# RMS and layer norms before products: turning undivided blocks by transposes, and applying the deviations behind the products

## The reference, cut to what matters

```
def rms_norm(x, g):
    y = xf * lax.rsqrt(jnp.mean(xf * xf, axis=-1, keepdims=True) + EPS)
    return (y * g.astype(jnp.float32)).astype(x.dtype)

def swiglu(h, w_gate, w_up, w_down):
    return (jax.nn.silu(h @ w_gate) * (h @ w_up)) @ w_down

def second_block(x, ...):
    h = swiglu(rms_norm(x, ff1_norm_pre[l]), ff1_w_gate[l], ff1_w_up[l], ff1_w_down[l])
    x = x + 0.5 * rms_norm(h, ff1_norm_post[l])
    h = hybrid_mixer(rms_norm(x, mix_norm_pre[l]), w_in[l], ...)
    x = x + rms_norm(h, mix_norm_post[l])
    h = swiglu(rms_norm(x, ff2_norm_pre[l]), ff2_w_gate[l], ff2_w_up[l], ff2_w_down[l])
    x = x + 0.5 * rms_norm(h, ff2_norm_post[l])
```

## Time and profile before

| | |
|---|---|
| median of the runs | 2370.24 us |
| profiled execution, its own time | 2373.72 us |
| its span, first to last instruction | 2371.5 us |
| TensorE matmul busy | 2320.2 us, 98% |
| VectorE, ScalarE, GpSimd busy | 890.4, 966.3, 988.9 us |
| mean granted TensorE clock | 0.996 |

### The profile page before, as it was taken

The page is one execution under the profiler, slowest core; times in us unless marked ns, Lnnn a source line. Parts: engine busy times, 40 slices in busy tenths (PEclk is TensorE's granted clock), DMA queues, the critical chain, the costliest instruction groups (busy, mean ns, idle before and its releaser), DMA issues.

```text
span 2371.5 us, 30775 instructions
## 1 busy us (share of the span) xinstructions
PE 2320.2 (98%) x11388; PEld 1906.8 (80%) x11388; DVE 890.4 (38%) x1181; ACT 966.3 (41%) x1643; POOL 988.9 (42%) x444
## 2 busy tenths in 40 slices
PE   8989999999999999999999999999999999999998
PEld 6868888888888878888887888888878768888887
DVE  6974444420453433444303322200536762323201
ACT  6775333321455553333314422222445565322212
POOL 6945444444322325444443444444343203444443
PEclk9999999999999999999999999999999999999999
DMA  5213322222212133222222222222321002322222
GB/s 187 72 49 104 114 97 97 97 98 94 84 63 68 58 115 107 98 97 97 90 96 89 94 94 96 97 98 98 142 72 62 28 15 76 106 97 97 95 94 95
DMA packets 58757, 215.20 MB, mean 91 GB/s; under 512 B 6448, under 2 KB 6448, under 8 KB 58416
## 3 DMA queue, kind: packets, MB, share of 16 engines
q1 hardware_dynamic: 55440, 199.83, 24.2%
q10 hardware_dynamic: 3232, 14.16, 1.6%
HBM read 211.86 MB, written 2.10 MB: 90 GB/s over the span
## 4 chain that ended last, share of the span: by engine, by line
PE 59%; issue 22%; POOL 10%; DVE 5%; ACT 3%; DMA 1%; POOLq 0%; SPq 0%; DVEq 0%; ACTq 0%
PE banks L510 12%; PE banks L512 12%; PE banks L511 12%; POOL wL L458 9%; PE banks L536 6%; PE banks L537 6%; PE banks L538 6%; DVE banks L1929 2%; PE banks L993 1%; POOL pool_sum L473 1%; PE banks L1037 1%; DMA raw<-ws 1%; PE banks L551 1%; ACT tmp L1661 1%; PE banks L945 0%
## 5 line engine op out<-in xcount | busy, mean ns | idle before, releaser
L458 POOL TENSOR_TENSOR wL<-raw,wH 128x1024 fp32r<-128x1024 f32 x369 | 898.1, 2436 | 1355.9 <-ACT wH L1202 1355.7
L1202 ACT ACTIVATE wH<-raw 128x1024 fp32r<-128x1024 f32 x371 | 393.5, 1061 | 1088.5 <-PE banks L512 598.6
L510 PE MATMUL banks<-xH,wH 128*128 128x512 f32 (+1 forms) x1976 | 762.5, 386 | 13.6 <-DVE xL L1751 10.8
L512 PE MATMUL banks<-xH,wL 128*128 128x512 f32 (+1 forms) x1976 | 756.1, 383 | 0.0
L511 PE MATMUL banks<-xL,wH 128*128 128x512 f32 (+1 forms) x1976 | 756.0, 383 | 0.0
L510 PEld LDWEIGHTS banks<-xH,wH 128*128 128x128 f32 x1976 | 371.8, 188 | 90.8 <-DVE wL L1756 10.8
L512 PEld LDWEIGHTS banks<-xH,wL 128*128 128x128 f32 x1976 | 371.8, 188 | 72.8
L511 PEld LDWEIGHTS banks<-xL,wH 128*128 128x128 f32 x1976 | 371.9, 188 | 72.0 <-issue 1.0
L536 PE MATMUL banks<-wH,hH 128*128 128x512 f32 x704 | 274.2, 389 | 3.5 <-DVE tmp L1888 3.5
L537 PE MATMUL banks<-wH,hL 128*128 128x512 f32 x704 | 273.9, 389 | 0.0
L538 PE MATMUL banks<-wL,hH 128*128 128x512 f32 x704 | 273.9, 389 | 0.0
(11 more groups left out here) (282 smaller groups left out, 2287.0 us busy)
## 6 DMA issues: line engine op xcount, KB each, us to landing
raw<-ws SPq DMA_DIRECT2D x371, 512.0 KB, 3.2
w1b<-w ACTq DMA_DIRECT2D x2, 2048.0 KB, 10.7
tmp<-rows ACTq DMA_DIRECT2D x7, 512.0 KB, 3.4
b_row<-rows ACTq DMA_DIRECT2D x5, 512.0 KB, 3.8
tmp<-xT SPq DMA_DIRECT2D x8, 256.0 KB, 7.3
xr<-xN ACTq DMA_DIRECT2D x1, 2048.0 KB, 8.6
out<-xr SPq DMA_DIRECT2D x4, 512.0 KB, 2.6
pf<-pT ACTq DMA_DIRECT2D x2, 512.0 KB, 3.3
```

The costliest lines, as they stand in the source:

```text
L458: pool.tensor_tensor(wL[:, j, :], raw[:, j, :], fp(wH[:, j, :]), ALU.subtract).then_inc(low_ready, 1)
L510: pe.matmul(bank, wH[:, slot, cols], rh, start=start, stop=False)
L512: return pe.matmul(bank, wL[:, slot, cols], rh, start=False, stop=stop)
L1202: act.activation(wH[:, c % SLOTS, :], raw[:, c % SLOTS, :], ACT.Copy).then_inc(high_ready, 1)
```

## The change

At the four places a block is turned by plain transposes (`pe.transpose` with the identity), and `turner` and `turning_matrix` are gone.

- Layer norm at `ffn0`: ScalarE divides the block in place before it is turned (`divide_block`), and VectorE later only adds the bias row (`shift_block` for `finish_block`).
- The three RMS norms before a product: the undivided `xr` is turned as soon as VectorE has finished the block. `pre_block` still computes 1/deviation, but nothing before the product waits for it. TensorE later spreads the four columns over a row of 512 tokens in bank 3 (`spread`, four transposes of a column read 128 times), and VectorE copies it to `r_row` (`take_row`).
- The factor is applied behind the products: to the gate's bank by VectorE before silu (44 products of 128x512, new semaphore `gate_scaled`), in the mixer to the copied and turned items and to the rotary tables themselves, once. The up product stays unscaled. Its factor is applied at the layer's end: as `scale` in the square of `post_block`, and in `update_block` together with the gain row (`SCALE_OF`).
- Orders are changed: `pre_block` of blocks 1, or 2 and 3, stands later on ScalarE, and VectorE makes all casts of the first half before it takes in block 3.

```diff
             def turn_block(xname, q, src):
                 h = q // 2
-                pe.wait_ge(x_normed, QT * TURN[xname] + q + 1)
                 for n in range(KT):
                     bank = ps[TURN_BANKS[xname][h][n // 2]]
                     o = (n % 2) * 2 * P + (q % 2) * P
-                    if src is divided:
-                        mm = pe.transpose(bank[:, o:o + P], xg[:, q, n * P:n * P + P], cc("ident"))
-                    else:
-                        mm = pe.matmul(bank[:, o:o + P], src(q)[:, n * P:n * P + P], turner[:, q, :], start=True, stop=True)
+                    mm = pe.transpose(bank[:, o:o + P], src[:, q, n * P:n * P + P], cc("ident"))
...
+            def updated(xname, q):
+                if xname == "ff1_pre":
+                    pe.wait_ge(res_step, RES_STEPS[2] + q + 1)
+                else:
+                    name = {"mix_pre": "down2", "ff2_pre": "wout"}[xname]
+                    pe.wait_ge(block_taken, 8 * FULL[name] + 2 * q + 2)
+                turn_block(xname, q, xr)
+
+            def spread(name, xname):
+                for q in range(QT):
+                    pe.wait_ge(x_normed, QT * TURN[xname] + q + 1)
+                    mm = pe.transpose(ps[3][:, q * P:q * P + P], figure(name, q, 7).broadcast_to([P, P]), cc("ident"))
+                mm.then_inc(r_turned, 1)
...
-                gate_and_up(1, c0 + 2)
+                if inst < 2:
+                    gate_and_up(1, c0 + 2)
+                else:
+                    tile_product(ps[6][:], c0 + 2, (c0 + 2) % SLOTS)
+                    spread(*(("down1", "ff1_pre") if inst == 2 else ("wout", "ff2_pre")))
+                    tile_product(ps[7][:], c0 + 3, (c0 + 3) % SLOTS)
...
@@ scalar, layer_norm (ffn0) and pre_block
-                    unit_block(name, q)
+                    divide_block(name, q)
...
-                turning_matrix(name, q, 7)
+                act.sem_inc(x_normed, 1)
...
@@ scalar, down1 to gateup2
             pre_block("down1", "ff1_pre", 0)
+            high_tiles("ff1_pre", 0, 0, 2, gain="ff1_pre")
+            deviation("down1", 2)
+            high_tiles("ff1_pre", 0, 2, 4, gain="ff1_pre")
+            deviation("down1", 3)
             pre_block("down1", "ff1_pre", 1)
-            deviation("down1", 2)
-            high_tiles("ff1_pre", 0, 0, 2, gain="ff1_pre")
-            deviation("down1", 3)
-            high_tiles("ff1_pre", 0, 2, 4, gain="ff1_pre")
+            high_after(CHUNK["gateup2"] - 1)
+            high_tiles("ff1_pre", 1, 0, 4, gain="ff1_pre")
             pre_block("down1", "ff1_pre", 2)
             pre_block("down1", "ff1_pre", 3)
-            high_after(CHUNK["gateup2"] - 1)
-            high_tiles("ff1_pre", 1, 0, 4, gain="ff1_pre")
...
@@ vector, ffn
+                        else:
+                            dve.wait_ge(chunk_done, t * 4 + (c0 + 2 * j + 1))
+                            dve.wait_ge(h_made, t * 2 + (24 * inst + j + 1))
+                            dve.tensor_tensor(tmp[:, j, :], ps[4 + 2 * j][:], r_row[:], ALU.mult).then_inc(gate_scaled, 1)
...
@@ vector, mixer
+            take_row("mix_pre")
             take_item(0)
             take_item(1)
+            dve.wait_ge(rope_loaded, 16)
+            for a in range(2):
+                dve.tensor_tensor(ropeT[:, a, :], ropeT[:, a, :], r_row[:], ALU.mult).then_inc(rope_scaled, 1)
```

More of the change, by code:

```diff
@@ L263, in build_block @@
         x_turned = sem("x_turned")
+        r_turned = sem("r_turned")
+        r_ready = sem("r_ready")
+        gate_scaled = sem("gate_scaled")
         res_step = sem("res_step")
@@ L400, in build_block @@
             TURN_BANKS[n] = ((0, 1, 2, 3), (6, 7, 0, 1))
+        PRE_ROW = {n: i for i, n in enumerate(["ff1_pre", "mix_pre", "ff2_pre"])}
+        SCALE_OF = {"down2": "down1", "down3": "wout"}
         XV = {"in": 0, "mix0": KT, "ffn0": 3 * KT, "mix1": 5 * KT, "ff1_pre": 7 * KT, "mix_pre": 9 * KT,
@@ L912, in last_pair @@
                 begin_wo(1, range(LEAD))
-            first_chunks((ps[7], ps[6]), c0, "down0", "ffn0", centred("down0"), (4, 6), 3)
+            first_chunks((ps[7], ps[6]), c0, "down0", "ffn0", divided, (4, 6), 3)
             project(0, 0, 2)
@@ L1123, in _ @@
             first_chunks((ps[item_bank(0)], ps[item_bank(1)]), c0, "down2", "mix_pre", updated, (4, 8), 8)
+            spread("down2", "mix_pre")
             project_item(2)
@@ L1312, in post_block @@
                     act.wait_ge(chunk_done, CHUNK[name] + dict(COUNTS)[name])
-                act.activation(squares[:], banks[:, 2 * q:2 * q + 2, :].rearrange("p a b -> p (a b)"), ACT.Square,
-                               accum_out=figure(name, q, 3)).then_inc(post_sum, 1)
+                block = banks[:, 2 * q:2 * q + 2, :].rearrange("p a b -> p (a b)")
+                scale = figure(SCALE_OF[name], q, 7) if name in SCALE_OF else 1.0
+                act.activation(squares[:], block, ACT.Square, scale=scale, accum_out=figure(name, q, 3))\
+                    .then_inc(post_sum, 1)
                 act.wait_ge(post_sum, QT * FULL[name] + q + 1)
@@ L1968, in _ @@
             for q in range(QT):
-                finish_block("down0", q)
+                shift_block("ffn0", q)
             def scan(p, n, h, i, qt, o, w):
@@ L2039, in _ @@
             add_block("down1", 2)
+            low_tiles("ff1_pre", 0, 0, 2, gain="ff1_pre")
             centre_block("down1", 2)
+            low_tiles("ff1_pre", 0, 2, 4, gain="ff1_pre")
+            finish_block("down1", 2)
             add_block("down1", 3)
-            low_tiles("ff1_pre", 0, 0, 2, gain="ff1_pre")
-            finish_block("down1", 2)
             centre_block("down1", 3)
-            low_tiles("ff1_pre", 0, 2, 4, gain="ff1_pre")
             finish_block("down1", 3)
@@ L2079, in take_item @@
                         dve.wait_ge(rope_low, r - 1)
-                    else:
-                        dve.wait_ge(rope_loaded, 16)
                     scale = DH ** -0.5 if name in ("dq", "nq") else 1.0
```

75 lines of the change are left out of this document (38 added, 37 removed).

## The result

The changed kernel takes 2380.91 us, median of 10 runs (2376.36 to 2387.12), against 2370.18 for the kernel before, measured beside it. The ratio is 1.0049, with a 95% interval of 1.004 to 1.0059: slower by 0.5%, 10.7 us. I had forecast 2377.7 in a range of 2366 to 2385, slower with a chance of 0.62. The profiled execution of the changed kernel has an own time of 2378.86 us and a span of 2377.0; its mean granted clock is 0.993, against 0.996 before.

The account below looks back on a forecast made before the run. TensorE, busy 98% of the span, was taken as the bound. Stage terms summed to +0.5 us at full clock, plus 7 for the clock: +7.5 on the median 2370.24, so 2377.7 us, range 2366 to 2385.

Parts of the forecast that it names:

- My sum: Whole kernel at full clock: all stage terms and the layer's end together, before any clock loss, +0.5 us.
- C's first wait: Between down2 and hybrid: TensorE's 3.12 us gap for VectorE's update of block 2 stays about 2.9 us.
- D: Stage from wout to gateup3: -1.8, spreading +0.43 and the fourth chunk's wait +2.9, together +1.5 us.
- The clock: All four stages: new gaps bring four low stretches of granted clock, one in each stage, +7 us.
- Stage A: From down0 to qkv: ScalarE scales blocks in place, first product 0.7 us later, then shorter turns, -1.2 us.
- Stages B and D, block 3: down1 to gateup2, wout to gateup3: TensorE waits 2.0 and 2.5 us before block 2's turn; terms -1.5, -1.8.
- The fourth chunk: After down1 and after wout: TensorE idles 2.9 us each for a chunk behind late sums and row load.
- Theory 1 or 2: Set up after the result: the loss is the granted clock, or it is the new waits, whatever the clock does.
- The second: Rival, all stages: clock holds or drops twice at most, +0.5 to +4.0 us, 2370.7 to 2374.2; chance 0.27.
- The third: Rival, after down1 and wout: the fourth chunk is in time and the clock holds, -5.3 us, 2364.9; chance 0.08.
- The fourth: Rival, all turns: TensorE's saved work falls on the path in full, -13.6 us, 2356.6; chance 0.03.
- The fifth: Rival, every stage: clock stays low because turns do not hold it up, +14.1 us, 2384.3; chance 0.05.

Follow-up runs that it names:

- fillers: Changed kernel plus idle matmuls, or in one run transposes, in TensorE's gaps at the four stages, all waits kept: 2374.72, 2375.19 and 2374.48 us.
- The first fillers: Changed kernel plus idle matmuls in its gaps at the four stages, some sharing a bank with open sums: 2374.72 us, ratio 1.0022.
- Block 3's runs: Changed kernel with VectorE taking block 3 in one or two tile pairs sooner, row load not moved: 2375.88 us, ratio 1.002.
- the orders alone: Changed kernel with the gain row's load ahead of the late sums and block 3 taken in sooner, no idle matmuls: 2368.21 us, ratio 0.9985.
- both orders mended and the gaps filled: Changed kernel with row load and block 3 earlier, idle matmuls in remaining waits, turns after down2 not held for block 2's update: 2359.13 us, ratio 0.9953.

## Why the prediction was right, and where not

**Sign and mechanism: right; how the loss divides, only in part.** No change at full clock and a loss by the clock was the forecast. At full clock, by the runs' mean times (2381.9 and 2370.6), the kernels stand at 2381.9 - 19.8 = 2362.1 and 2370.6 - 10.3 = 2360.3, +1.8; by the two profiled spans, 2377.0 x 0.993 = 2360.4 and 2371.5 x 0.996 = 2362.0, -1.6. My sum was +0.5. But both readings take off all the low time of the changed kernel, also what fell into its waits, and so flatter it. With fillers the mean clocks of the two kernels are level, and the changed kernel stands 4.1, 4.7 and 4.0 us above the kernel before. By that reading my sum at full clock was some 4 us short. Of these, C's first wait has 0.8; D is not among them, since from its first turn to the fourth chunk's product it takes 29.8 us (1996.04 to 2025.85) against 28.4 before (to 2020.69), +1.4 where I had +1.5:

```profile
1992.30 2.05 PE L551 MATMUL banks<-turner,xr 128*128 128x128 f32 x16
```

The rest is not traced, and the fillers may have a share in it.

**The clock: +7 forecast, +9.5 by the runs' mean clocks, about 6 of it given back by fillers.** I had one low stretch of 3.5 us in each of the four stages. The profile has one of 3.4 in A, 6.8 in B and in C, none in D. Against the low time the term is undersized by the double stretches, against what fillers gave back it is about right, and which stage drops was not foreseen. One stretch in each of four stages was a choice between bounds, so that the size came near is in part luck.

**Stage A: -1.2 forecast, -1.0 alone, which the interval does not tell from nothing.** The first product comes 4.46 us behind the first turn (5.15 before), where I had it later by 0.7: all 16 transposes of blocks 0 and 1 follow each other in 1.91 us, so block 1's turn did not wait for its division, for which I had put 0.8.

**Stages B and D, block 3.** Waits before block 2's turn: 1.76 us in B (2.0 forecast, 1302.1 to 1304.1), 3.78 in C (3.9), 2.19 in D (2.5); before block 3's in B 1.02 (1.1). C's first wait grew to 3.69 from 3.12, where I had 2.9. In B block 1's turn did not wait at all (1.5 forecast), and the first product came at 1295.98, not 1297.8.

**The fourth chunk: 2.9 in B and in D.** In D 2.54, and the mechanism (load behind late sums, then halving, table, high part, split) is the one I chained; moving the load alone gave 5.0 us, some 3 of them by the clock. In B it was 0, which the prediction itself had named as a sign of being wrong, and this is the step that failed: the sum was made at full clock and then the clock was added. A stretch of low clock between the two makes TensorE late for a chunk that is late itself, so the two cover each other. The first fillers show it: with B at full clock and every order as it was, the wait is 2.76 us, 2.44 of it filled. Block 3's runs show the other side: once TensorE is earlier, the chunk's wait is back (2.96 us in D, 2.76 in B).

**Theory 1 or 2.** Both, and they are not separate sums. Fillers alone gave back 6.2, 5.7 and 6.4 us with every wait in place; the orders alone gave back 12.7, in shorter waits and in clock (0.9917 to 0.9947), since the waits are also the gaps ahead of the low stretches.

**Rivals.** The second (clock drops twice at most) fails on the three stages. The third names the right wait, but without it alone the kernel is at 2375.9, not 2364.9: I had put the clock's return on it, and the low stretches lie ahead of that chunk. The fourth, all of TensorE's saving on the path, was 24 us off as it stood (2356.6 against 2380.9); with both orders mended and the gaps filled, 2359.1 comes near its 2356.6. The fifth is refuted by the transposes in the gaps.

## What to carry to other kernels

When work before a product gets shorter, read what stood in its shadow: here the order of casts, late sums and a row's load was made for the old length, and mending two orders was worth more (12.7 us) than the change cost (10.7). Where TensorE must wait several times in short order, put idle matmuls or transposes into the waits, ahead of the wait itself and in a bank that holds nothing; then check that the gap, and not the work behind it, is filled. And do not add a clock loss to a wait that lies behind it: count whichever ends later.

## What had not been expected

The granted clock of one kernel differs between its runs, and the time with it: the changed kernel ran from 2376.36 us at a clock of 0.994 to 2387.12 at 0.990, 10.8 us over a step of 0.004, of which the clock's own share is 9.5. A profile shows one such run only. The two waits of A were followed by 0.51 in the changed kernel (0.60 and 1.30 us), by 0.53 with both orders mended (0.60 and 1.12) and by 1.00 with stage A alone changed (0.60 and 1.09).
